# Expert weights of a decoder layer: each 1 MB chunk loaded by two transfers of half its columns

## What is computed

```python
logits = h @ w_router + b_router
top_v, top_e = top_k(logits, 4)                 # 4 of 32 experts for each token
gate = softmax(top_v)
for each expert e, on the tokens that chose it:
    hu = x @ w_up[e] + b_up[e]                  # w_up[e] is 1024 x 2048, float32
    g  = min(hu[:, 0::2], 7)
    u  = clip(hu[:, 1::2], -7, 7)
    y  = ((u + 1) * g * sigmoid(1.702 * g)) @ w_down[e] + b_down[e]   # 1024 x 1024
out[token] += gate * y
```

## Time and profile before

| | us |
|---|---|
| Median of 3 runs | 1679.96 |
| Lowest, highest | 1672.06, 1681.13 |
| The profiled execution's own time | 1679.47 |
| Its span in the trace | 1677.8 |

### The profile page before, as it was taken

How to read it: one execution, slowest core, us unless ns; L and a number is a source line. 1 busy time by engine, 2 the same in 40 slices (tenths; PEclk the granted TensorE clock), 3 DMA queues, 4 the chain that set the end, 5 groups by cost and what they waited for, 6 DMA issues and landing times.

```text
span 1677.8 us, 22266 instructions
## 1 busy us (share of the span) xinstructions
PE 1441.0 (86%) x6497; PEld 1036.9 (62%) x6498; DVE 1240.8 (74%) x1279; ACT 939.0 (56%) x864; POOL 297.0 (18%) x416
## 2 busy tenths in 40 slices
PE   5993687889988999999999999999999999999850
PEld 3761476554536666666776676666777767767630
DVE  0246562855548999999789999999978897898835
ACT  0111322612116877887578778878756776787622
POOL 5303989800300001000000110001000001000000
PEclk8996795769898999999999999999999999999975
DMA  9974254132418999999989999999978999799734
GB/s 352 363 248 145 90 196 168 23 125 83 159 45 316 389 401 396 389 407 400 352 301 395 401 401 386 399 396 400 396 280 324 381 404 367 270 405 402 280 117 134
DMA packets 124956, 498.54 MB, mean 297 GB/s; under 512 B 21105, under 2 KB 46274, under 8 KB 91026
## 3 DMA queue, kind: packets, MB, share of 16 engines
q1 hardware_dynamic: 104146, 454.56, 70.6%
q0 software_dynamic: 14768, 29.16, 5.1%
q10 hardware_dynamic: 5984, 14.11, 2.4%
HBM read 499.43 MB, written 26.25 MB: 313 GB/s over the span
## 4 chain that ended last, share of the span: by engine, by line
PE 44%; DVE 24%; issue 14%; ACT 7%; SPq 6%; DMA 2%; DVEq 1%; ACTq 0%; POOL 0%; POOLq 0%
PE psum L537 42%; DVE w_lo L1790 14%; SPq L391 5%; ACT w_hi L1244 4%; ACT arena L1204 2%; PE psum L540 2%; DMA early<-in_pages 1%; DMA arena<-y_dram 1%; DVE arena L1814 1%; DVE x_split L1850 1%; DVE y_part L1856 1%; DVE arena L1434 1%; DVE arena L1435 1%; DVE arena L1336 1%; SPq L388 1%
## 5 line engine op out<-in xcount | busy, mean ns | idle before, releaser
L1790 DVE TENSOR_TENSOR w_lo<-arena,w_hi 128x2048 fp32r<-128x2048 f32 x352 | 795.4, 2288 | 106.4 <-ACT w_hi L1244 105.4
L1244 ACT ACTIVATE w_hi<-arena 128x2048 fp32r<-128x2048 f32 x344 | 652.9, 1914 | 251.3 <-PE psum L537 248.9
L537 PE MATMUL psum<-arena 128*128 128x64 f32 (+8 forms) x2514 | 518.7, 380 | 48.0 <-DMA arena<-in_w_in 17.6
L537 PEld LDWEIGHTS psum<-arena 128*128 128x128 f32 (+3 forms) x2514 | 354.3, 204 | 215.7 <-issue 162.4
L537 PE MATMUL psum<-w_lo,x_split 128*128 128x512 f32 x1408 | 401.9, 407 | 59.6 <-DVE w_lo L1790 54.0
L537 PE MATMUL psum<-w_hi,x_split 128*128 128x512 f32 x1628 | 441.3, 399 | 9.0 <-DVE x_split L1850 5.9
L537 PEld LDWEIGHTS psum<-w_lo,x_split 128*128 128x128 f32 x1408 | 255.2, 190 | 173.0 <-DVE w_lo L1790 126.3
L537 PEld LDWEIGHTS psum<-w_hi,x_split 128*128 128x128 f32 x1628 | 306.2, 191 | 73.2 <-issue 6.1
L2009 POOL DMA_INDIRECT y_dram<-y_part,arena x32 | 39.0, 1218 | 1016.8 <-DVE y_part L1856 732.0
L540 PE MATMUL psum<-arena 128*128 128x128 f32 (+4 forms) x501 | 80.3, 313 | 66.3 <-ACT arena L1088 30.2
L1336 DVE TENSOR_REDUCE arena<-early 128x32 f32<-128x2048 f32 x16 | 35.8, 2280 | 109.0 <-DMA early<-in_pages 109.0
(11 more groups left out here) (231 smaller groups left out, 750.2 us busy)
## 6 DMA issues: line engine op xcount, KB each, us to landing
arena<-in_w_up SPq DMA_DIRECT2D x256, 1024.0 KB, 7.6
arena<-in_w_down SPq DMA_DIRECT2D x128, 1024.0 KB, 7.3
early<-in_pages SPq DMA_DIRECT2D x160, 128.0 KB, 2.9
arena<-in_w_in ACTq DMA_DIRECT2D x23, 512.0 KB, 7.2
arena<-in_pages POOLq DMA_DIRECT2D x32, 128.0 KB, 7.3
early<-in_pages POOLq DMA_DIRECT2D x32, 128.0 KB, 6.6
arena<-in_pages SPq DMA_DIRECT2D x32, 128.0 KB, 2.2
early<-in_w_plg SPq DMA_DIRECT2D x1, 4096.0 KB, 15.1
```

Of the source, the lines that this page charges most:

```text
L537: return TE.matmul(out, lhsT, rhs, start=start, stop=stop, skip_group_check=True)
L1244: SE.activation(w_hi[:, (8 + t) % 3], chunk_in[(8 + t) % 6], ACT.Copy).then_inc(hi_ready, 1)
L1790: VE.tensor_tensor(w_lo[:, at], chunk_in[buf], w_hi[:, at].bitcast(f32), SUB).then_inc(lo_ready, 1)
```

## The change

Each chunk is loaded by two transfers instead of one. The first fills columns 0 to 1023 of the chunk's tile, the second columns 1024 to 2047; each moves 512 KB in 128 rows of 4 KB. Of a w_up chunk the halves are the left and the right half of its rows, which are 8 KB apart in memory; of a w_down chunk they are its two blocks of rows. Both add 16 to the buffer's semaphore, so all thresholds on `w_here` double. There are 768 transfers of weights where there were 384; the bytes, the buffers and the order stay.

```diff
--- before.py
+++ after.py
@@ -460,12 +460,13 @@
 
             def weights_to(e, c, buf):
 
-                if c < 8:
-                    dst, src = chunk_in[buf], up[e, c] if isinstance(e, int) else up[bass.ds(e, 1), c].rearrange("e p n -> (e p) n")
-                else:
-                    dst = chunk_in[buf].rearrange("p (a n) -> p a n", a=2)
-                    src = down[e, c - 8] if isinstance(e, int) else down[bass.ds(e, 1), c - 8].rearrange("e p a n -> (e p) a n")
-                sp.dma_start(dst, src).then_inc(w_here[buf], 16)
+                for n in range(2):
+                    cols = slice(n * D, n * D + D)
+                    if c < 8:
+                        src = up[e, c, :, cols] if isinstance(e, int) else up[bass.ds(e, 1), c, :, cols].rearrange("e p n -> (e p) n")
+                    else:
+                        src = down[e, c - 8, :, n] if isinstance(e, int) else down[bass.ds(e, 1), c - 8, :, n].rearrange("e p n -> (e p) n")
+                    sp.dma_start(chunk_in[buf][:, cols], src).then_inc(w_here[buf], 16)
 
             def weights(e, c):
                 weights_to(e, c, c)
@@ -970,7 +971,7 @@
                                 last = mm(psum[0:CAP, 4 + c, :], x[:, 2 * q + a], w[:, at, a * D + c * 512:a * D + c * 512 + 512],
                                           q == 0 and n_pass == 0 and a == 0, False)
                         last.then_inc(chunk_used, 1)
-                    pe.wait_ge(w_here[buf], i * 32 + ((first + 3) // 6 * 16 + 16))
+                    pe.wait_ge(w_here[buf], i * 64 + ((first + 3) // 6 * 32 + 32))
                     for a, c in ((0, 0), (0, 1), (1, 0), (1, 1)):
                         last = mm(psum[0:rows, 4 + c, :], act_sb[:, 6 + a, 0:rows], raw[:, a * D + c * 512:a * D + c * 512 + 512], False, a == 1)
                     last.then_inc(chunk_used, 1)
@@ -1191,7 +1192,7 @@
 
             def high(s, at, buf):
 
-                act.wait_ge(w_here[buf], s // 6 * 16 + 16)
+                act.wait_ge(w_here[buf], s // 6 * 32 + 32)
                 act.wait_ge(chunk_used, s + 1)
                 SE.activation(w_hi[:, at], chunk_in[buf], ACT.Copy).then_inc(hi_ready, 1)
 
@@ -1239,7 +1240,7 @@
                 n = PER if end < NE else 4
 
                 def part(t):
-                    act.wait_ge(w_here[(8 + t) % 6], i * 32 + ((8 + t) // 6 * 16 + 16))
+                    act.wait_ge(w_here[(8 + t) % 6], i * 64 + ((8 + t) // 6 * 32 + 32))
                     act.wait_ge(chunk_used, s + (t + 1))
                     SE.activation(w_hi[:, (8 + t) % 3], chunk_in[(8 + t) % 6], ACT.Copy).then_inc(hi_ready, 1)
```

## The result

| | before | after |
|---|---|---|
| median of the runs, us | 1679.31 (1672.06 to 1681.13) | 1699.38 (1687.96 to 1701.58) |
| after / before | | 1.0126, interval 1.0075 to 1.0177 |
| profiled execution, own time / span, us | 1679.5 / 1677.8 | 1699.09 / 1697.4 |
| mean granted TensorE clock | 0.913 | 0.913 |

The change costs 20 us (1.3%), where 7 were forecast. Executions of one kernel spread over about 1%, so a difference is read from the ratio with its interval; this interval lies clear of 1. The two profiled spans differ by 19.6 us, so the pair of traces shows the whole of it.

What follows compares the result with a forecast made beforehand. It took the engines' loop as the bound in light experts, barely ahead of the weight stream, and PE in heavy ones. Two long light runs, 3.0 + 4.4 = +7.4 us on 1679.5, gave 1687 us; range 1676 to 1704.

Steps and rivals of the forecast that it cites:

- The price of a cut row and of a completion: Weight loads: cutting rows adds 0.07 us a w_up chunk, 16 more completions 0.01 us a chunk; 0.6 us an expert taken.
- The rival of a latency paid in turn: Weight loads: each further transfer adds 2.2 us, 56 us an expert, kernel some 2400 us; chance 0.01.
- a price of each transfer: Rival for queued weight loads: transfers have their own price, 2.9 us an expert, up to 1737 us, 1704 at half; chance 0.14.
- a change that does nothing: Rival for w_up loads: half rows might still travel as before, packet count and time staying; chance 0.02.
- step (6): Light experts: 0.6 us delay each adds up, less the margin; +3.0 first long run, +4.4 second, 0 short runs and heavy experts.
- The DMA engines never rest: Light experts: DMA engines busy 100 to 101% of 32.42 us, so the weight stream was taken to have almost no spare time.
- My term of +7.4 us: Two long runs of light experts: total delay reaching the kernel's end, 3.0 plus 4.4 us.
- hidden anyway: Rival in light experts: the stream has spare time and 0.6 us fits; period stays 32.42, 1679.5 to 1682 us; chance 0.24.
- part (1): w_up packets: an 8 KB row takes 0.310 us, two 4 KB rows 0.318; +0.07 us a w_up chunk, nothing for w_down.
- the 419 GB/s of the y_dram loads: Kernel's last loads, 4 KB rows 16 KB apart: taken as nearest to the half loads, 0.04 us a chunk, low end 0.3.
- step (4): SP's queue: 768 loads have room, 14 of 32.4 us; second half issued at most 0.6 us later, there in time.

Runs made afterwards that it cites:

- the probe: Kernel before, then SP alone loads 24 w_up chunks in each of nine ways; running queue: whole 2.49, adjacent rows or halves 2.56 us a chunk.
- contiguous blocks: Against the changed kernel: two transfers per chunk still, but each w_up half is a contiguous 512 KB block with adjacent 4 KB rows; 1.0014 of before.
- one transfer: Against the kernel before: each w_up chunk still one 1 MB transfer, but read as adjacent rows of 4 KB, two per partition; 1.0009 of before.

## Why the prediction was right, and where it was wrong

**Right.** Slower, with the mechanism in the right place: in light experts the stream of weights passed the loop of engines. The heavy experts kept their time but for 1.8 us and the stages ahead of them did too, the waits for loads rose (1.8 us to 56.5 on tile w_hi), DMA grew in the chain. The price of a cut row and of a completion, +0.08 us a w_up chunk, is what the probe measured (2.49 to 2.56) and the changed kernel shows in its gaps between landings in a full queue (2.48 to 2.56). A light expert was to take 32.9 to 33.1 us and took 33.5. SP had the room forecast: ten issues of 0.346 us in the 12 us after 656. The rival of a latency paid in turn is refuted by every run here; a price of each transfer by the contiguous blocks (+0.14%, within the interval); a change that does nothing by the packet count.

**Wrong, step (6) and the reading ahead of it.** "The DMA engines never rest", so a delay of 0.6 us "adds up" in each light expert. The runs with one transfer and with contiguous blocks put just such a delay on the stream, 8 x 0.08 = 0.64 us an expert, in the second with 12 more completions. The first long run grew by 0.1 and 1.4 us, not by 3.0, and the stretch with the second by 0.0 and 1.2 us, not by 4.4; the 1.2 lie in its heavy part, and its light experts kept their 32.4. The stream had at least 0.64 us an expert to spare, with engines shown as busy for 100%. Gaps between landings show where (last completion to last completion, means of 13 light experts): before, chunks 8 to 11 land 3.68, 2.90, 2.76 and 2.76 us apart, against 2.56 for rows of 4 KB in a full queue, 1.9 us in sum, of which the token rows explain a part. The share was 0.99 at 338 GB/s and 1.00 at 410, so it cannot tell a full stream from a slowed one. My term of +7.4 us should have been 0 to +2.5, the case "hidden anyway", had rows of a half been adjacent.

**Wrong, the missing term.** In part (1) I took the price of a half row from the earlier trace rows, whose rows are adjacent, and dismissed distance by the 419 GB/s of the y_dram loads, 16 KB apart. That 419 is from a queue that has been running, and for such a queue it is right. The same row starts with some 8 us at 177 to 380 GB/s, which I passed over; whether they are the same effect, no run tests. Each light expert lets the queue run low once, and there rows that are apart are read slowly for 8 us. Chunks 5, 6 and 7 of the changed kernel land 3.47, 3.14 and 3.96 us apart on the mean of 13 light experts: 10.57 us instead of 3 x 2.56. Over an expert: after, 33.5 us = 12 x 2.56 + 2.8, with the stream as the bound; before, 32.4 = 8 x 2.48 + 4 x 2.56 + 2.3, of which at least 0.64 was to spare and so at most 1.7 were token rows and the dip. The slow stretch thus costs at least 2.8 - 1.7 = 1.1 us more than before; the probe, measured apart from this, says 1.1 to 1.3 for a start on an empty queue. The packets add 0.64, and at least as much was spare, which leaves the 1.1 us by which the period grew. Over the long stretches that is 8.1 + 10.2 us in 18 light experts, 1.0 each on the mean (the first of the second run still takes 32.4), and 1.8 in the heavy part between: the +20.1 measured.

**Wrong, step (4).** "The first has 1.4 us of other data ahead of it" was worked out from when the last part of a load landed. At that time some DMA engines were already dry: their share is 0.83 from 660.9 to 661.8 us before, and 0.75 from 664.8 to 666.2 after (windows above). One load's parts don't end together; the sixteen completions of chunk 4 before spread from 660.96 to 662.99 us. For the time of a landing it did no harm; as a picture of the queue it hid the very moment that decides.

**Luck.** The size of the result lay inside the range only because a rival with another mechanism, a price of each transfer, had been let in at half its price. That rival is not what happened.

**Open.** Why rows that are apart are slow just after the queue ran low, and not later: the runs show that it is so, not what in memory or in the DMA engines does it. Why 16 KB is no worse than 8. How the gathers lengthen the stretch. Whether the low queue or the burst of issues behind it sets it off. Whether loads issued earlier at chunk 5, so that the queue never runs low, would take the loss away was not tried.

## What to carry to other kernels

Cut a contiguous transfer into contiguous blocks, not into column halves: the first was nearly free here (1.0014), the second cost 1.3%. Blocks put a weight in another place; the kernel that shows the 1.0014 left the rest of the program as it was, so the cost of matching it is not shown. A DMA share of 100% is no proof that the stream is the bound; take some of its load away (here the gathered rows) and see whether the period moves. And price a change of access pattern where the queue runs low, not only in a full one: one such moment per expert made nearly the whole loss.

## What the runs showed of the hardware that was not expected

- Rows of 4 KB that lie 8 KB apart run at the rate of adjacent ones in a full queue (2.56 us a MB for both), but cost 1.1 to 1.3 us more after each start on an empty one. At 16 KB the kernel lost as much (1.0124).
- In such a stretch the DMA engines show 98 to 99% busy at 251 to 338 GB/s, against 410 to 415 else.
- Packets of 4 KB instead of 8 cost 3% of the rate (2.56 against 2.49 us a MB), and a second completion and issue for the same MB nothing more that can be seen.
- A matmul whose 128 columns of weights are read with a step of four floats took 417 ns, with a step of two 283 (at a granted clock of 0.91 and 1.00).
